# Attention scores from high and low parts of q and k, in three one-pass matmuls, in a two-layer hybrid trunk

## The reference, cut to what matters

```
x = x + 1/2 * SwiGLU_1(RMSNorm(x))                 # 1024 -> 2816 -> 1024
proj = RMSNorm(x) @ w_in                           # 1024 -> 5888: q, k, v of A, B, C and three gates
q, k: RMSNorm per head of 64, then rotary embedding
C (4 units of 2 heads): (softmax(q1 k1') - lam * softmax(q2 k2')) v, causal
A (4 heads, 2 units):   softmax(q k') v, causal (one block of 256 keys)
B (4 heads, 2 units):   softmax(q k') v in a window of 128 keys, with a sink
x = x + (sum_i sigmoid(g_i) * (branch_i @ P_i)) @ w_out
x = x + 1/2 * SwiGLU_2(RMSNorm(x))
```

## Time and profile before

| | before |
|---|---|
| time, median of 3 runs | 1165.22 us (1165.12 to 1165.5) |
| span of the profiled execution | 1163.5 us |
| TensorE matmuls busy | 1152.0 us, 99% |
| TensorE weight loads busy | 969.3 us, 83% |
| VectorE busy | 773.4 us, 66% |
| ScalarE busy | 646.3 us, 56% |
| granted TensorE clock, mean over the span | 1.000 |

### The profile page before, as it was taken

The page is one execution under the profiler, slowest core; times in us unless marked ns, Lnnn a source line. Parts: engine busy times, 40 slices in busy tenths (PEclk is TensorE's granted clock), DMA queues, the critical chain, the costliest instruction groups (busy, mean ns, idle before and its releaser), DMA issues.

```text
span 1163.5 us, 16200 instructions
## 1 busy us (share of the span) xinstructions
PE 1152.0 (99%) x6011; PEld 969.3 (83%) x6011; DVE 773.4 (66%) x1036; ACT 646.3 (56%) x964; POOL 71.9 (6%) x81
## 2 busy tenths in 40 slices
PE   7999999999999999999999999999999999999998
PEld 6888888888888888888888888888877888888887
DVE  4766656778747676566677656667786495766555
ACT  6545445657773565454555445456576745554542
POOL 3100000220100000000040000002110000000000
PEclk9999999999999999999999999999999999999999
DMA  9965554544534665555567555536454445656520
GB/s 311 286 197 197 182 182 145 175 152 146 181 123 167 217 212 186 181 183 194 173 161 241 181 182 185 193 100 209 145 169 159 159 151 191 223 182 192 192 86 36
DMA packets 138364, 207.34 MB, mean 178 GB/s; under 512 B 6818, under 2 KB 99028, under 8 KB 138292
## 3 DMA queue, kind: packets, MB, share of 16 engines
q1 hardware_dynamic: 137444, 205.55, 53.7%
q0 software_dynamic: 752, 0.79, 0.8%
q10 hardware_dynamic: 96, 0.02, 0.0%
HBM read 205.29 MB, written 1.05 MB: 177 GB/s over the span
## 4 chain that ended last, share of the span: by engine, by line
PE 96%; ACT 1%; DVE 1%; DMA 1%; issue 0%; SPq 0%; ACTq 0%; DVEq 0%
PE bank L506 27%; PE bank L474 17%; PE bank L478 16%; PE bank L477 16%; PE bank L510 14%; PE bank L488 1%; PE bank L690 1%; DMA raw<-in_ffn_w_up 1%; PE bank L660 1%; PE bank L676 1%; PE bank L675 1%; PE bank L704 0%; PE bank L706 0%; PE bank L705 0%; DVE probs L1252 0%
## 5 line engine op out<-in xcount | busy, mean ns | idle before, releaser
L1080 DVE TENSOR_TENSOR w_low<-raw,w_high 128x1024 fp32r<-128x1024 f32 x388 | 472.0, 1235 | 305.2 <-ACT w_high L832 304.4
L832 ACT ACTIVATE w_high<-raw 128x1024 fp32r<-128x1024 f32 x388 | 403.7, 1056 | 329.7 <-PE bank L510 173.5
L506 PE MATMUL bank<-xT,w_high 128*128 128x512 f32 x1392 | 492.2, 398 | 2.6 <-DVE work L1114 2.0
L510 PE MATMUL bank<-xT,w_low 128*128 128x256 f32 x1408 | 390.4, 280 | 0.0
L506 PEld LDWEIGHTS bank<-xT,w_high 128*128 128x128 f32 x1392 | 261.2, 188 | 67.4 <-issue 2.1
L510 PEld LDWEIGHTS bank<-xT,w_low 128*128 128x128 f32 x1408 | 263.9, 189 | 1.4
L474 PE MATMUL bank<-w_high,xT 128*128 128x512 f32 (+1 forms) x448 | 177.2, 395 | 0.1
L478 PE MATMUL bank<-w_low,xT 128*128 128x512 f32 (+1 forms) x448 | 171.8, 383 | 0.0
L477 PE MATMUL bank<-w_high,xT 128*128 128x512 f32 (+1 forms) x448 | 171.1, 382 | 0.0
L474 PE MATMUL bank<-w_high,oT_high 128*128 128x512 f32 x416 | 163.6, 393 | 0.0
L478 PE MATMUL bank<-w_low,oT_high 128*128 128x512 f32 x416 | 162.6, 391 | 0.0
(11 more groups left out here) (127 smaller groups left out, 770.1 us busy)
## 6 DMA issues: line engine op xcount, KB each, us to landing
raw<-in_w_in SPq DMA_DIRECT2D x92, 512.0 KB, 4.5
raw<-in_ffn_w_down SPq DMA_DIRECT2D x88, 512.0 KB, 4.2
raw<-in_ffn_w_gate SPq DMA_DIRECT2D x87, 512.0 KB, 4.1
raw<-in_ffn_w_up SPq DMA_DIRECT2D x87, 512.0 KB, 5.0
raw<-in_w_out SPq DMA_DIRECT2D x16, 512.0 KB, 4.4
raw<-in_w_branch_c SPq DMA_DIRECT2D x8, 512.0 KB, 4.3
raw<-in_w_branch_b SPq DMA_DIRECT2D x4, 512.0 KB, 4.0
raw<-in_w_branch_a SPq DMA_DIRECT2D x4, 512.0 KB, 4.0
```

Of the source, the lines that this page charges most:

```text
L506: return nc.tensor.matmul(bank[n][:, :], w_high[:, slot, column(k, n)], xT[:, k], start=k == 0, stop=False)
L510: return nc.tensor.matmul(bank[n][:, 0:S], weights[:, slot, column(k, n)], xT_high[:, k], start=start, stop=k == KB - 1)
L832: act.activation(w_high[:, slot], raw[:, in_slot, (p % 2) * 1024:(p % 2) * 1024 + 1024], ACT.Copy).then_inc(sem["high_ready"], 1)
L1080: dve.tensor_tensor(w_low[:, slot], raw[:, FILL_SLOT[p // 2], (p % 2) * 1024:(p % 2) * 1024 + 1024], w_high[:, slot].bitcast(F32), ALU.sub ...
```

## The change

The turned q and k are split as the weights are. ScalarE's `copy_rope` writes the rounded high part into oT_high (raising the new semaphore rope_high for each of its two copies); a new VectorE step `rope_low` subtracts it from the bank into oT_low and then raises rope_copied. Its place in VectorE's loop is behind the rope of a chunk and ahead of the pair's own `low`, at the turn's position plus 5. The blocks used are first % 8 on, so turns 3 and 4 overwrite those of turns 1 and 2. A score matmul in fp32 becomes three float32r matmuls that accumulate, high by high, low by high and high by low, alternating between the two heads of the unit. Turn 2 moves from TensorE position 15 to 14. The columns of the gates tile that held q and k are no longer written by the copies.

```diff
-ROPE_TURNS = [(0, 4, 10), (4, 4, 15), (8, 4, 25), (12, 3, 31)]
+ROPE_TURNS = [(0, 4, 10), (4, 4, 14), (8, 4, 25), (12, 3, 31)]
...
-        def qk_blocks(first, count):
+        def qk_blocks(tile, first, count):
...
-            base, per_half, c0 = (0, 4, 0) if first < 8 else (8, 2, 1024) if first < 12 else (12, 2, 1536)
-            half, n = divmod(first - base, per_half)
-            return gates[:, half, c0 + n * S:c0 + (n + count) * S]
+            block = first % 8
+            return tile[:, block:block + count, :]
...
-                q32, k32 = qk_blocks(qb, 1), qk_blocks(kb, 1)
-                for t in range(2):
-                    rows = slice(DH * t, DH * t + DH)
-                    nc.tensor.matmul(bank[4 + t][:, 0:P], q32[rows, 0:P], k32[rows, 0:P], start=True, stop=True)
-                    last = nc.tensor.matmul(bank[4 + t][:, P:3 * P], q32[rows, P:S], k32[rows, :], start=True, stop=True)
+                (q_high, k_high), (q_low, k_low) = ([qk_blocks(tile, n, 1)[:, 0] for n in (qb, kb)] for tile in (oT_high, oT_low))
+                for out, queries, keys in ((slice(0, P), slice(0, P), slice(0, P)), (slice(P, 3 * P), slice(P, S), slice(0, S))):
+                    for n, (q, k) in enumerate(((q_high, k_high), (q_low, k_high), (q_high, k_low))):
+                        for t in range(2):
+                            rows = slice(DH * t, DH * t + DH)
+                            last = nc.tensor.matmul(bank[4 + t][:, out], q[rows, queries], k[rows, keys], start=n == 0, stop=n == 2)
...
-                    last = act.activation(qk_blocks(first + b, w), bank[6 + b // 2][:, 0:w * S], ACT.Copy)
-                last.then_inc(sem["rope_copied"], 1)
+                    act.activation(qk_blocks(oT_high, first + b, w), bank[6 + b // 2][:, 0:w * S].rearrange("p (k s) -> p k s", k=w), ACT.Copy
+                                   ).then_inc(sem["rope_high"], 1)
...
+            def rope_low(layer, n):
+
+                first, count, _ = ROPE_TURNS[n]
+                for b in range(0, count, 2):
+                    w = min(2, count - b)
+                    dve.wait_ge(sem["rope_high"], value("rope_high", layer, 2 * n + b // 2 + 1))
+                    last = dve.tensor_tensor(qk_blocks(oT_low, first + b, w), bank[6 + b // 2][:, 0:w * S].rearrange("p (k s) -> p k s", k=w),
+                                             qk_blocks(oT_high, first + b, w).bitcast(F32), ALU.subtract)
+                last.then_inc(sem["rope_copied"], 1)
...
+                    for n, (_, _, pos) in enumerate(ROPE_TURNS):
+                        if m == pos + RING - 1:
+                            rope_low(layer, n)
```

More of the change, by code:

```diff
@@ L108 @@
     "proj_done": len(PROJ), "proj_read": len(PROJ), "head_squares": 5, "head_totals": 6, "heads_scaled": 6, "tables_ready": 1, "rope_done": 5,
-    "rope_turned": 4, "rope_copied": 4,
+    "rope_turned": 4, "rope_high": 8, "rope_copied": 4,
     "scores_done": 8, "scores_masked": 8, "exps_ready": 8, "probs_ready": 8, "probs_turned": 8,
```

## The result

| | before | after |
|---|---|---|
| time, median | 1165.36 us (1165.12 to 1166.32, 4 runs) | 1182.93 us (1181.9 to 1183.19, 4 runs) |
| span of the profiled execution | 1163.5 us | 1180.1 us |

The ratio of the times is 1.0148 (95% interval 1.0136 to 1.0159): the change makes the kernel 17.6 us slower. The profiled execution is the fastest of the four (1181.9); what follows divides its 16.6 us.

A forecast was written before the change was run, and what follows sets the result against it. TensorE, busy 1152.0 of 1163.5 us, was taken as the bound; stalls 10.9, clock 2.8 and score matmuls 0.5 make 14.2 us, span 1177.7, and with 1.7 us outside it 1179.4 us, range 1173.6 to 1186.

The forecast's parts named there:

- more waits than I count: Rival: further waits at turn 4 (1.7 us a layer) or position 14; 1181 to 1184 us, chance 0.12.
- Score matmuls: TensorE's six one-pass pairs a unit take 1.09 us, 0.03 more than now; 0.5 us over 16 units.
- The load's price: In the score matmuls, a narrow pair can't be shorter than its weight load, 0.11 us; three cost 0.33.
- the two bounds: Narrow score pairs: 2.2 us less than now over all if loads were hidden, 5.5 more at the fp32 rate.
- The rival at the fp32 rate: Rival: narrow one-pass score matmuls run at the fp32 rate, 5.0 us more, 1184.4 us; chance 0.24.
- Loads overlap matmuls: Score pairs: loads overlap matmuls of the same row group; the rival without overlap adds 7.4 us, 1186.8, chance 0.03.
- Turn 3: Position 25: turn_probs of unit 2 waits for subtractions behind VectorE's mask of unit 3; 5.48 and 5.45 us, together 10.9.
- Positions 10 and 14: TensorE at turns 1 and 2: VectorE's subtractions end in time, so no wait; 0.9 us of cover at position 14.
- The clock: After each of turn 3's two pauses TensorE restarts at the lower clock, 1.4 us lost each, 2.8 us in all.
- Turn 4: Position 31, turn_probs of unit 4: nothing counted, since TensorE comes 5.5 us later and VectorE only about 3.
- the case without turn 3's pause: As the engines stand before the change, turn 4 would wait 1.7 us a layer for its subtractions.

The follow-up runs named there:

- e8_narrow_widened: e1_early with the narrow group of the score matmuls widened from 128 to 256 keys, results overwritten by the wide group: 1167.93 us, ratio 1.0022.
- e4_kept_busy: The changed kernel with 44 idle matmuls of zeros ahead of turn_probs of unit 2, inside the 5.3 us wait: 1178.47 us, ratio 1.0112.
- e3_before_mask: The changed kernel with the rope_low loop moved whole above that of mask_scores in VectorE's order: 1175.7 us, ratio 1.0094.
- e2_turn3_early: The changed kernel with only turn 3's subtractions moved, into the rope of chunk 4; turn 4's stay behind the mask of unit 5: 1171.14 us, ratio 1.0056.
- e1_early: The changed kernel with rope_low earlier on VectorE: turn 3's inside the rope of chunk 4, the others ahead of the mask: 1167.73 us, ratio 1.0019.

## Why the prediction was right, and where it was short

The direction, the mechanism and its place were as forecast: 1179.4 us (1173.6 to 1186) against 1182.93, a change of 14.2 forecast and 17.6 measured. What was missing is turn 4 and the size of the clock's loss. The measured time even lies in the 1181 to 1184 us of the rival *more waits than I count*, which had a chance of 0.12 and named turn 4 and the reason, that VectorE doesn't gain on TensorE after the stall; its price of 1.7 us a layer was too high, and the clock made up the rest. Point by point:

- *Score matmuls*, 0.5 us: right. 0.03 us a unit, 0.4 us over 16. The load's price, between the two bounds, was the right one. The rival at the fp32 rate is out: the narrow pairs step at 0.11 us and not at 0.21, and in e8_narrow_widened twice the columns cost 0.01 us a pair. The Trainium skill's four passes (FP8 and Floating Point Precision, "TensorE Precision Notes") are in the rows, but counting them would have given 2.6 us of gain, of which none came.
- *Loads overlap matmuls*: right. Wide pairs step at 0.12 us (e8_narrow_widened) with 0.107 of columns in them; loads that had to wait for matmuls of their own rows would give 0.22.
- *Turn 3*, 10.9 us: right, 10.6. The order was read rightly to the instruction: the subtractions ran from 285.57 where 285.38 was worked out, in a trace that runs 0.2 us later there. The 0.3 us too many are mostly the hand-over: the subtractions end at 286.85 and L690 starts 0.15 us behind, not 0.25.
- *Positions 10 and 14*, no wait: right (VectorE's subtractions for turn 1 end at 238.8, the transposes follow at 239.87 without one).
- *The clock*, 2.8 us: the mechanism was right, the term too small. 3.8 us in the profiled execution, the fastest of four; the other three were 1.0 to 1.3 us longer at a mean granted clock of 0.994 instead of 0.996, and e4_kept_busy gives 3.5 to 4.3. I had also read from the end of the trace that the clock falls within 3 us of rest. In the changed kernel it fell after 3.0 and 4.6 us, and in e3_before_mask once not at all in a pause of 3.6. The restarts seen, two in the changed kernel and one at the start of the kernel before, lost different times (1.5, 2.3 and 1.4 us), so one row at the start was no measure of its size. (At the start the steps of 0.43 us tell the lower level; the windows of the granted clock read 1.00 there.)
- *Turn 4*, nothing: this step failed. I wrote that VectorE would come only about 3 us later while TensorE comes 5.5 later. It came 6.4 us later in low 34 and still in the mask of unit 5, while TensorE came 7.0 later. What I overlooked is on ScalarE: the copy of unit 3's probabilities stands ahead of the exponentials of unit 4 and of high 34, and waits for TensorE's own turn_probs. Before, then after:

```profile
292.32 0.49 ACT L989 ACTIVATE probsT<-bank 128x384 f32<-128x384 f32 x1 [1.32 <-PE bank L690]
296.10 1.23 DVE L1080 TENSOR_TENSOR w_low<-raw,w_high 128x1024 fp32r<-128x1024 f32 x1 [0.34 <-ACT w_high L832]
```

```profile
299.31 0.49 ACT L989 ACTIVATE probsT<-bank 128x384 f32<-128x384 f32 x1 [3.06 <-PE bank L690]
302.53 1.22 DVE L1080 TENSOR_TENSOR w_low<-raw,w_high 128x1024 fp32r<-128x1024 f32 x1 [2.10 <-ACT w_high L832]
```

The copy moved 7.0 us, as TensorE did; high 34 comes behind it, and VectorE's low 34 waits for high 34. So VectorE gained 0.6 us on TensorE and not 2.5, and of the 1.7 us a layer 1.0 was left: 2.0 us in all. The 1.7 us a layer for the case without turn 3's pause was too low as well: e2_turn3_early has 2.4, since the earlier subtraction itself delays VectorE, by 0.9 us in e1_early.

## What to carry to other kernels

A step that is cheap on a half-idle engine costs what stands in front of it in that engine's program order at the moment when somebody waits: work it out from the timeline, instruction by instruction, and put the step where its input lands, not at the end of a loop body. Before trading passes of a small matmul for more instructions, look at the step of a row of that width: here no pair stepped under 0.11 us, the step of a weight load, and below that fewer columns bought nothing. When a pause of the busiest engine is found, ask of each neighbour whether it runs ahead on its own or waits for a result of the paused engine, for only the first kind catches up.

## What the runs showed of the hardware that was not expected

- A restart at the lower clock is no fixed price. Pauses of 5.3 us were followed by 2.9 and 4.6 us of work at 1.2 GHz in one execution, and two pauses of 3.6 us by none and by 3.4 us of it, which began only 0.6 us after the matmuls had started again. In the changed kernel, 44 matmuls of zeros held the clock at 2.4 GHz through 5 us.
- On 64 rows, matmuls of two heads that alternate start together (one row for a pair above), in one pass as in fp32; the step of a pair is 0.11 us at 128 moving columns and 0.12 at 256, where the columns alone take 0.05 and 0.107 (128 and 256 at 2.4 GHz).
